# Query projection of a PEER layer on one core: its columns cut into sides of 232 and 312, the last two normed tiles transposed inside the first two query units

## What is computed

```python
h = h + mix
h = h + peer_ffn(rmsnorm(h, norm_ffn_w), w_query, sub_keys, expert_u, expert_v)

def peer_ffn(x, w_query, sub_keys, expert_u, expert_v):
    q = (xt @ w_query).reshape(n, PEER_HEADS, 2, PEER_KEY_DIM)
    s = jnp.einsum('nhpd,hpkd->nhpk', q, sub_keys)
    s1, i1 = lax.top_k(s[:, :, 0], PEER_TOPK)
    s2, i2 = lax.top_k(s[:, :, 1], PEER_TOPK)
    ...
    act = jax.nn.gelu(jnp.einsum('nd,nhed->nhe', xb, u), approximate=False)
    return jnp.einsum('nhe,nhed->nd', gb * act, expert_v[eb])
```

## Time and profile before

| | us |
|---|---|
| median of 3 runs | 1868.88 |
| lowest and highest | 1867.03, 1873.43 |
| the profiled execution, device time | 1871.53 |
| its span, first to last instruction | 1869.8 |
| TensorE busy | 1798.9 |
| VectorE busy | 1383.7 |
| ScalarE busy | 715.1 |
| POOL busy | 673.4 |
| mean granted clock of TensorE | 0.975 |

### The profile page before, as it was taken

One profiled execution on the slowest core, in us unless ns is written; L12 is line 12 of the kernel. 1 busy time (PEld: TensorE's weight loads), 2 busy tenths in 40 slices (PEclk: granted clock), 3 DMA queues, 4 the chain that ended last, 5 costly groups with the idle time before them and its releaser, 6 DMA issues.

```text
span 1869.8 us, 29423 instructions
## 1 busy us (share of the span) xinstructions
PE 1798.9 (96%) x11505; PEld 1748.5 (94%) x11505; DVE 1383.7 (74%) x2531; ACT 715.1 (38%) x1252; POOL 673.4 (36%) x438
## 2 busy tenths in 40 slices
PE   7998988979899999999999999999999999999998
PEld 6997888769899999999999999999999999999997
DVE  4976887663599999999876566527778788888753
ACT  5545335442433343343343333333333333333342
POOL 3000000000001577768776776852344333333100
PEclk9988998879999999999999999999999999999999
DMA  7211001044302487989988999999999999999831
GB/s 212 77 38 46 32 9 44 23 107 148 105 25 91 163 285 264 301 292 312 307 303 290 311 322 314 308 343 358 331 384 381 348 340 354 355 342 344 313 116 37
DMA packets 190706, 424.33 MB, mean 227 GB/s; under 512 B 11162, under 2 KB 119222, under 8 KB 180320
## 3 DMA queue, kind: packets, MB, share of 16 engines
q1 hardware_dynamic: 153256, 287.47, 44.5%
q0 software_dynamic: 37312, 134.97, 20.5%
HBM read 360.76 MB, written 62.06 MB: 226 GB/s over the span
## 4 chain that ended last, share of the span: by engine, by line
PE 58%; DVE 16%; issue 2%; DMA 2%; POOL 1%; ACT 1%; DVEq 0%; POOLq 0%; ACTq 0%
PE psum L1296 29%; PE psum L1275 21%; PE psum L1263 3%; PE psum L902 3%; DVE junk L2424 2%; DMA act<-act_dram 2%; DVE besti L2287 1%; DVE sring L2291 1%; DVE besti L2299 1%; DVE best L2295 1%; DVE best L2283 1%; PE psum L907 1%; DVE WR L1793 1%; DVE oh L2414 1%; DVE eqx L2357 1%
## 5 line engine op out<-in xcount | busy, mean ns | idle before, releaser
L1275 PE MATMUL psum<-xT,WS 128*128 128x416 f32 x3072 | 594.7, 353 | 2.8 <-POOL WS L842 2.8
L1296 PE MATMUL psum<-AR,WS 128*128 128x416 f32 x3072 | 582.1, 351 | 4.6 <-DVE AR L2495 4.6
L1296 PEld LDWEIGHTS psum<-AR,WS 128*128 128x128 f32 x3072 | 575.4, 188 | 11.4 <-DVE AR L2495 5.3
L1275 PEld LDWEIGHTS psum<-xT,WS 128*128 128x128 f32 x3072 | 572.1, 188 | 8.5 <-POOL WS L842 4.0
L842 POOL TENSOR_TENSOR WS<-RAWP,WS 128x1024 fp32r<-128x1024 f32 x128 | 311.1, 2441 | 707.1 <-ACT WS L1693 610.0
L833 POOL DMA_INDIRECT rowg<-in_expert_v,idx x128 | 181.0, 1414 | 320.6 <-DVE acc L2438 312.8
L907 PE MATMUL psum<-xT,WR 128*128 128x280 f32 (+1 forms) x1968 | 276.0, 300 | 10.4 <-DVE xT L1820 7.2
L907 PEld LDWEIGHTS psum<-xT,WR 128*128 128x128 f32 x1968 | 264.4, 196 | 12.0 <-DVE xT L1820 7.8
L1703 ACT ACTIVATE WS<-RAWP 128x1024 fp32r<-128x1024 f32 x128 | 135.6, 1059 | 332.0 <-PE psum L1296 321.7
L2488 DVE TENSOR_TENSOR WS<-RAWP,WS 128x1024 fp32r<-128x1024 f32 x128 | 156.6, 1224 | 115.1 <-ACT WS L1703 115.1
L1730 ACT ACTIVATE actA<-psum 128x416 f32<-128x416 f32 x128 | 66.4, 519 | 401.5 <-PE psum L1275 395.2
(11 more groups left out here) (372 smaller groups left out, 1610.5 us busy)
## 6 DMA issues: line engine op xcount, KB each, us to landing
RAWP<-in_expert_u SPq DMA_DIRECT2D x64, 1024.0 KB
RAWP<-in_expert_v SPq DMA_DIRECT2D x64, 1024.0 KB
act_dram<-actA SPq DMA_DIRECT2D x128, 208.0 KB
gate_dram<-gblk SPq DMA_DIRECT2D x26, 1024.0 KB
act<-act_dram SPq DMA_DIRECT2D x64, 416.0 KB
Gt<-gate_dram SPq DMA_DIRECT2D x16, 1664.0 KB
RAW<-in_w_in SPq DMA_DIRECT2D x8, 1024.0 KB, 5.4
RAW<-in_w_query SPq DMA_DIRECT2D x8, 1024.0 KB, 8.3
```

What stands on the lines that cost most here:

```text
L1275: last = mm(bank[e % 2][:, 0:TD], ws(e)[:, pw, kt * P:(kt + 1) * P], xT[:, px, kt, TSP:TPE], start=(kt == 0 and i == 0), stop=(kt == KT - ...
L1296: last = mm(bank[dt][:, 0:TD], ws(NK + e)[:, pw, dt * P:(dt + 1) * P], AR[:, e % 4, pa, :], start=(e == 0 and i == 0), stop=(e == NK - 1 a ...
```

## The change

The token columns of the query units are cut at 232, where tile 1 ends, and no longer at 272: `QSIDE` has the first column and the number of columns of each side. Side 0 then needs tiles 0 and 1 alone, side 1 has 312 columns. The wait ahead of unit 0 is for `xlow` of tile 1. The transposes of tile 3 stand behind unit 0 as before, those of tile 4 between the two halves of unit 1. ScalarE takes the copies of tiles 0, 1 and 2 ahead of the squares of tiles 2, 3 and 4, and the root of each tile right behind its square. The order of VectorE is the same.

```diff
-PHALF = TPE // 2
+QSIDE = [(0, PT[2][0]), (PT[2][0], TPE - PT[2][0])]
...
-                            hw = PHALF if kind == "query" else HALF
+                            c0, hw = QSIDE[side] if kind == "query" else (side * HALF, HALF)
                             last = mm(bank[u % 4][:, 0:hw], W[:, pw, kt, m * P:(m + 1) * P],
-                                      xT[:, px, kt, side * hw:(side + 1) * hw], **go)
+                                      xT[:, px, kt, c0:c0 + hw], **go)
...
-            def between_query(n):
-
-                if n < 2:
-                    norm_tile(2, 3 + n)
-                if n == 1:
+            def inside_query(n, half):
+
+                if (n, half) == (0, 1):
+                    norm_tile(2, 3)
+                elif (n, half) == (1, 0):
+                    norm_tile(2, 4)
+                elif (n, half) == (1, 1):
                     V.wait(pe, "xlow", 2, NTP - 1, 1)
 
-            V.wait(pe, "xlow", 2, 2, 1)
+            V.wait(pe, "xlow", 2, 1, 1)
...
-                    fn(qT[:, ct % 2, half * PHALF:(half + 1) * PHALF], bk[:, 0:PHALF], ACT.Copy, "unit", u)
+                    c0, c = QSIDE[half]
+                    fn(qT[:, ct % 2, c0:c0 + c], bk[:, 0:c], ACT.Copy, "unit", u)
...
             root(2, 1)
-            square(2, 2)
             xhigh(2, 0)
-            square(2, 3)
-            root(2, 2)
-            xhigh(2, 1)
-            square(2, 4)
-            root(2, 3)
-            xhigh(2, 2)
-            root(2, 4)
-            xhigh(2, 3)
-            xhigh(2, 4)
+            for t in range(2, NTP):
+                square(2, t)
+                root(2, t)
+                xhigh(2, t - 1)
+            xhigh(2, NTP - 1)
```

More of the change, by code:

```diff
@@ L905, in unit_half, with linear @@
                             m, side = query_unit(n) if b == first["query"] else (n // 2, n % 2)
-                            hw = PHALF if kind == "query" else HALF
+                            c0, hw = QSIDE[side] if kind == "query" else (side * HALF, HALF)
                             last = mm(bank[u % 4][:, 0:hw], W[:, pw, kt, m * P:(m + 1) * P],
-                                      xT[:, px, kt, side * hw:(side + 1) * hw], **go)
+                                      xT[:, px, kt, c0:c0 + hw], **go)
                 if half:
                     T.op(last, "unit", u)
-            def linear(b, between=lambda n: None):
+            def linear(b, between=lambda n: None, inside=lambda n, half: None):
                 V.wait(pe, "low", b)
                 for u in range(UNIT0[b], UNIT0[b + 1]):
-                    unit_half(b, u, 0)
-                    unit_half(b, u, 1)
+                    for half in range(2):
+                        unit_half(b, u, half)
+                        inside(u - UNIT0[b], half)
                     between(u - UNIT0[b])
@@ L1237, in _ @@
                 i = b - first["query"]
-                linear(b, *([between_query] if i == 0 else []))
+                if i == 0:
+                    linear(b, inside=inside_query)
+                else:
+                    linear(b)
                 score(2 * i)
```

## The result

The changed kernel took 1862.09 us, the median of 9 runs (1850.97 to 1867.61), beside 1867.46 for the kernel before on the same chip (9 runs, 1865.64 to 1873.89). The ratio is **0.9946, 95% interval 0.9928 to 0.9964**, 10.1 us less; measured once more it was 0.9951 (0.9927 to 0.9974), 9.2 us less. The forecast was 6.6 us, a ratio of 0.9965. The measured ratio, put on the 1868.88 that the forecast started from, gives 1858.8 us, just under its range of 1859 to 1867.5. So the sign and the terms at the first query block came out as forecast, and the gain is some 3 us larger than the sum. How much larger is itself uncertain: the medians differ by 5.4 us in the first measurement, the means by 8.3, and the means of the repeat by 8.7. Single runs of the changed kernel lie over 16 us, and what spreads them is part of the answer.

A forecast was written before the change was run, and what follows sets the result against it. TensorE, busy 96% of the span, was taken to bound the kernel. A 7.54 us gain at the first query block less 0.9 in the other seven gave 6.6, so 1868.88 - 6.6 = 1862.2 us, range 1859 to 1867.5.

The forecast's parts named there:

- The idle time ahead of unit 0: First query block: TensorE's transposes start 0.15 us sooner, and its 4.70 us of idling before unit 0 vanishes.
- Unit 0: First query block: 24 matmuls at 0.112 us take 2.69 instead of 4.39 us, gaining 1.70.
- The wait for tile 4: First query block: TensorE's wait for xlow of tile 4 falls from 1.60 to 0.21 us, gaining 1.39.
- The cover: Inside the first units: xn of tiles 3 and 4 is ready 1.3 and 0.8 us before TensorE comes for it.
- Units 2 and 3 with their scores: First query block: 48 matmuls of 312 instead of 272 columns lose 0.83 us, the scores' wait 0.04.
- The seven blocks: Other query blocks: 12.29 against 12.15 us each, 0.13 lost in each, 0.9 us in all.
- the first (a floor of 0.120): Rival: a 232-column matmul costs as much as a 256-column one, 3.6 us gained, 1865.3; chance 0.20 with the softer floor.
- the third (the price of plain float32): Rival: in side 0's units, float32r matmuls under 256 columns cost as plain float32, 102 us slower, 1965; chance 0.12.
- the second (given back downstream): Rival: later POOL waits grow or xn of tile 4 is late, costing 1.5 to 4 us, about 1865; chance 0.13.
- the clock's 1.3 us: Part of unit 0's 1.70 us gain: without the idle stretch before it, nothing lowers TensorE's clock.
- the 2.8 us for POOL stay: Up to the end of the first expert pass: TensorE's waits for POOL remain 2.8 us.
- every wait is between engines that have moved alike: From the first gather on: TensorE and VectorE are tied together, the smaller shift of 6.6 us counts, and waits stay unchanged.

The follow-up runs named there:

- before_again: The kernel before, unedited, measured and profiled once more: ratio 0.9994 (0.9975 to 1.0013) against itself.
- after_spread_fill: The changed kernel with the 2 MB hf load cut in five and 14 unused 416-column matmuls ahead of the second pass: ratio 0.9957 to the kernel before.
- before_plus3: The kernel before with 3 unused 416-column matmuls added late in the first expert pass: ratio 0.9991.
- after_plus8: The changed kernel with 8 unused 416-column matmuls added behind expert 124 of the first pass: ratio 0.9958 to the kernel before.
- order_only: The kernel before with only ScalarE's new order (copies ahead of the next square, root behind its square): ratio 0.9974.
- split_only: The kernel before with sides of 232 and 312 and the wait for tile 1, old ScalarE order, tile 4 behind unit 1: ratio 0.9970.
- late_wait: The changed kernel with the old wait ahead of unit 0, for xlow of tile 2 instead of tile 1: ratio 0.9972 to the kernel before.
- even_sides: The changed kernel with sides of 272 and 272 and the wait for tile 2: ratio 0.9957, and 0.9972 in its second measurement, to the kernel before.
- sides_128_416: The changed kernel with sides of 128 and 416 columns: ratio 1.0043 (1.0018 to 1.0067) to the kernel before.
- before_spread: The kernel before with the 2 MB hf load of the second expert pass cut in five: ratio 0.9993.
- after_spread: The changed kernel with the 2 MB hf load of the second expert pass cut in five: ratio 0.9937 to the kernel before, median 1854.85 us.
- late_look: One more profile of the same code as late_wait; no ratio given.

## Why the prediction was right, and where its size was off

**The terms of the first block.** Against the trace that it read, nearly every one holds.

- The idle time ahead of unit 0: unit 0 starts 5.65 - 0.78 = 4.87 us sooner; forecast 0.15 + 4.70.
- Unit 0 takes 481.48 - 478.71 = 2.77; forecast 2.69. The gain is 1.62, not 1.70.
- The wait for tile 4: unit 2 starts at 485.82, 7.76 us behind the start of tile 2's transposes; forecast 7.54. The 0.22 are matmuls that cost 0.115 (24 in 2.77) or 0.119 (12 in 1.43) when they stand between transposes, and not 0.112.
- The cover: `xn` of tile 3 is done at 478.79 + 1.28 = 480.07 and TensorE comes at 481.48, for tile 4 482.63 and 483.56. That is 1.4 and 0.9; forecast 1.3 and 0.8.
- Units 2 and 3 with their scores: 485.82 to 495.72 is 9.90 against 8.98, a loss of 0.92; forecast 0.83 + 0.04.
- The seven blocks: (118.65 - 17.78) - (124.95 - 25.04) = 0.96; forecast 0.9. The 0.112 held.
- Sum 7.26 for 7.54, and 6.30 for 6.6 at the first pass. POOL's waits stayed at 2.8, and from there to the second pass nothing was given back: 787.19 - 780.91 = 6.28.

Two prices of plain float32 were read a little low: the matmul of 8 columns is spaced 0.112 within its run, and that of 256 columns (1.67 - 0.38) / 6 = 0.215 and not 0.209, since the last one lasts 0.38. Neither changes a term of the sum.

Of the rivals, the first (a floor of 0.120) and the third (the price of plain float32) are refuted by the rows of 232 and of 128 columns; the second (given back downstream) by the 6.28.

**The step that failed** is the clock's 1.3 us in the term of unit 0. It was read from one execution and taken as a property of the kernel. Six traces of the same code give 124.95 to 126.45 for the first pass, 125.92 in the mean: the changed kernel is 7.3 sooner, since it has no idle time there for the clock to fall behind and is 118.6 in all its traces. The same holds, less clearly, for "the 2.8 us for POOL stay": in two of five traces of before the first pass took 2 us longer (before_again waited 4.4 us for POOL, not 2.8), and in one of the four whose code is the changed kernel's up to there (after_spread_fill). At the start of the second pass the mean of before is 788.9 (five traces; before_plus3 has added work), of after 781.4 (four): **7.5 us**, where 6.6 were forecast.

**And one term was put at nothing:** the start of the second pass. The prediction held that from the first gather on every wait is between engines that have moved alike. They have, but behind TensorE's 2.6 us of idle time there the clock and the pace were not the same: the first 528 matmuls took 100.8 us in the mean of before (five traces, 98.48 to 102.47) and 98.5 in all three of the changed kernel, 2.3 less. That the change brings this about, and not chance, is not shown: before_again had the 98.48 too, and after_plus8 lost it. The rest of the pass gives 482.1 (four traces of before) and 483.0 (two of after), which for two and four traces that spread over 9 us is no difference. 7.5 + 2.3 - 0.9 = 8.9, beside the 10.1 and 9.2 measured by the ratios and the 8.3 and 8.7 by the means. The same count for the others, start of the second pass plus 528 against 889.7 for before, beside the measured ratio:

```
kernel           by the traces   measured
order_only        3.5 sooner      4.9 (2.4 to 7.3)
split_only        5.1             5.6 (2.2 to 9.2)
late_wait         4.9 (2 traces)  5.2 (1.9 to 8.6)
even_sides        6.5             6.6 (two runs)
after              9.8            9.6 (two runs)
sides_128_416     8.6 later       8.0 later (3.4 to 12.5)
```

All six agree within 1.4 us, and the five that are not in the table (before_spread, before_plus3, after_spread, after_spread_fill, after_plus8) within 2.5. Most rest on a single trace, the intervals are wide, and the count leaves out the mixer and the rest of the second pass, where the traces scatter by more than that. What the chip's clock and pace do in a given execution stays open: which of 3.4 and 6.8 us (or nothing) follows an idle stretch, and which of the two paces a pass takes. It is shown that they do so in unchanged code, and that the low clock is not what sets the pace.

The profiled pair alone would have misled the other way: 1871.53 and 1867.61 are 3.9 us apart, because in the profiled execution after, the mixer took 0.6 us longer, the stall near 1360 us took 4.05 instead of 2.34, the clock was low behind it (1360.3 to 1367.1), and the pace fell to the 188.9 of before.

## What to carry to other kernels

Price an idle stretch of TensorE by its own length plus what the clock takes behind it, and read that second part from several executions, since one trace shows one draw: here 1.3 or 2.7 us behind 4.4, and nothing or 1.6 behind 2.4. Where two operands bound a matmul, split it so that the short part just reaches the time of its weights (232 columns), since below that (128) the partner pays for columns that nobody saves. And compare stages from a common mark inside the program, because the time of a whole execution can hide 6 us of local gain behind the luck of an earlier stage or a later pass.

## What was unexpected of the hardware

- The same idle time in the same code (4.42 us) was followed by 3.4 us at 1.2 GHz in two traces and by 6.8 us in four; 2.19 us ahead of the same unit by 3.4 in two (order_only, late_wait) and by none in two (late_look, even_sides_b).
- Matmuls of 416 columns ran at 186.7 or 188.9 ns in the second pass, for hundreds in a row, changing only at a stall, with the granted clock at 1.00 in both. Worth 7 us a pass of 3072; what decides is open.
- The same mixer code had TensorE at 1.2 GHz for 65 us in one execution (after_spread) and 89 in another (after_plus8), and reached the end of the output blocks at 471.3 and 478.4 us.
- A float32r matmul of 128 columns took 0.112 us, as one of 232 did; one of 272 took 0.1266 (median or mean from start to start).
